# Two blocks on one core: one norm in place of two between the blocks, and other PSUM banks in the mLSTM recurrence

## What is computed

```python
x = x + 0.5 * swiglu_ffn(rmsnorm(x, ffn1_norm), ...)
x = x + hybrid_mixer(rmsnorm(x, mix_norm), ...)
x = x + 0.5 * swiglu_ffn(rmsnorm(x, ffn2_norm), ...)
x = rmsnorm(x, final_norm)                    # end of the first block
h = rms_norm(x, norm_pre_g)                   # start of the second
u_a, z_a, q, k, v, o, z_b, gates, g_a, g_b = split(h @ w_in)
y_a = pooled(u_a) ... * silu(z_a)
h_fwd, h_bwd = mlstm_direction(...), flip(mlstm_direction(flip ...))
y_b = rms(h_fwd + h_bwd) * g * sigmoid(o) * silu(z_b)
merged = sigmoid(g_a + b0) * (y_a @ w_a) + sigmoid(g_b + b1) * (y_b @ w_b)
out = x + rms_norm(merged @ w_out, norm_post_g)
```

## Time and profile before

| | |
|---|---|
| runs, us | 1773.84, 1777.64 (median), 1782.02 |
| profiled execution, us | 1782.81 |
| its span, us | 1780.9 |
| mean granted TensorE clock | 0.969 |
| TensorE matmuls, busy | 1695.4 us, 7980 |
| DVE / ACT / GpSimd busy, us | 691.9 / 628.9 / 655.1 |

### The profile page before, as it was taken

The page is one execution under the profiler, slowest core; times in us unless marked ns, Lnnn a source line. Parts: engine busy times, 40 slices in busy tenths (PEclk is TensorE's granted clock), DMA queues, the critical chain, the costliest instruction groups (busy, mean ns, idle before and its releaser), DMA issues.

```text
span 1780.9 us, 22491 instructions
## 1 busy us (share of the span) xinstructions
PE 1695.4 (95%) x7980; PEld 1386.7 (78%) x7980; DVE 691.9 (39%) x1149; ACT 628.9 (35%) x929; POOL 655.1 (37%) x282
## 2 busy tenths in 40 slices
PE   7999999999999999999999989889888999999997
PEld 6888888888876678888888877667676778887886
DVE  4333330235327644333330127473736332372222
ACT  5322222234136553332222234334343433244432
POOL 3444444443330034444444434222222223444444
PEclk9999999999998899999999989899999999999999
DMA  4322222243220012222222222111111112332222
GB/s 159 105 94 94 96 100 99 95 155 93 71 83 13 1 36 95 95 94 94 94 100 101 95 71 71 61 70 60 59 59 52 66 48 83 118 99 90 95 95 95
DMA packets 41954, 149.25 MB, mean 84 GB/s; under 512 B 4784, under 2 KB 4912, under 8 KB 41648
## 3 DMA queue, kind: packets, MB, share of 16 engines
q1 hardware_dynamic: 40112, 142.36, 23.4%
q10 hardware_dynamic: 1792, 6.19, 1.1%
HBM read 145.39 MB, written 2.10 MB: 83 GB/s over the span
## 4 chain that ended last, share of the span: by engine, by line
PE 69%; issue 22%; POOL 4%; DVE 3%; ACT 1%; DMA 0%; POOLq 0%; DVEq 0%; SPq 0%; ACTq 0%
PE ps L499 15%; PE ps L501 15%; PE ps L500 15%; PE ps L601 4%; PE ps L603 4%; PE ps L602 4%; POOL w_lo L445 4%; PE ps L759 1%; PE ps L771 1%; PE ps L781 1%; PE ps L520 1%; PE ps L1084 1%; PE ps L1083 1%; PE ps L1082 1%; PE ps L527 1%
## 5 line engine op out<-in xcount | busy, mean ns | idle before, releaser
L445 POOL TENSOR_TENSOR w_lo<-w_raw,w_hi 128x1024 fp32r<-128x1024 f32 x262 | 633.9, 2420 | 992.1 <-ACT w_hi L1118 983.9
L1118 ACT ACTIVATE w_hi<-w_raw 128x1024 fp32r<-128x1024 f32 x260 | 275.5, 1060 | 967.5 <-PE ps L501 750.4
L499 PE MATMUL ps<-h_hi,w_hi 128*128 128x512 f32 x1496 | 595.3, 398 | 13.2 <-POOL w_lo L445 8.4
L500 PE MATMUL ps<-h_lo,w_hi 128*128 128x512 f32 x1496 | 586.5, 392 | 0.0
L501 PE MATMUL ps<-h_hi,w_lo 128*128 128x512 f32 x1496 | 586.3, 392 | 0.0
L499 PEld LDWEIGHTS ps<-h_hi,w_hi 128*128 128x128 f32 x1496 | 283.7, 190 | 76.8 <-issue 10.7
L501 PEld LDWEIGHTS ps<-h_hi,w_lo 128*128 128x128 f32 x1496 | 283.4, 189 | 60.2
L500 PEld LDWEIGHTS ps<-h_lo,w_hi 128*128 128x128 f32 x1496 | 283.8, 190 | 58.1
L601 PE MATMUL ps<-hid_hi,w_hi 128*128 (+1 forms) x352 | 137.0, 389 | 0.0
L603 PE MATMUL ps<-hid_hi,w_lo 128*128 (+1 forms) x352 | 136.9, 389 | 0.0
L602 PE MATMUL ps<-hid_lo,w_hi 128*128 (+1 forms) x352 | 136.9, 389 | 0.0
(11 more groups left out here) (303 smaller groups left out, 1679.5 us busy)
## 6 DMA issues: line engine op xcount, KB each, us to landing
w_raw<-in_units SPq DMA_DIRECT2D x262, 512.0 KB, 3.2
x<-in_x SPq DMA_DIRECT2D x4, 512.0 KB, 6.0
w<-in_w ACTq DMA_DIRECT2D x1, 2048.0 KB, 7.7
out<-scr SPq DMA_DIRECT2D x8, 256.0 KB, 2.0
scr<-proj ACTq DMA_DIRECT2D x8, 128.0 KB, 3.0
inv_count<-in_inv_count ACTq DMA_DIRECT2D x1, 1024.0 KB, 4.9
const<-in_const SPq DMA_DIRECT2D x1, 770.0 KB, 9.6
q_sc<-in_row_const ACTq DMA_DIRECT2D x1, 512.0 KB, 3.7
```

Of the source, the lines that this page charges most:

```text
L445: nc.gpsimd.tensor_tensor(w_lo[:, slot, :], w_raw[:, slot, :], w_hi[:, slot, :].bitcast(F32), ALU.subtract).then_inc(w_lo_done, 1)
L499: nc.tensor.matmul(ps[:, bank, :], whi, hi[:, k, :], start=(n == 0), stop=False)
L500: nc.tensor.matmul(ps[:, bank, :], whi, lo[:, k, :], start=False, stop=False)
L1118: nc.scalar.activation(w_hi[:, slot, :], w_raw[:, slot, :], ACT.Copy).then_inc(w_hi_done, 1)
```

## The change

1. **One norm between the blocks.** FFN2 now ends as FFN1 does: its stream is split raw, with the gain `g_both` = final gain times pre gain. The gates unit and four units of head 0 (`NRAW`) run on this raw stream and are multiplied with `r_row` by DVE as they are taken (`raw_take`). Two sums are made at once: of the squares, and of the squares times the final gain squared (in `r_row` as scratch, `add_square`); two column sums in bank 5 follow the first unit of head 0, and `inverse_of_both` makes from them the inverse root of the first norm (`x_col`) and the product of both (`r_col`). The spread of the roots goes into the middle of the next unit (`amid`), into bank 6.
2. **The normalised stream** `n_hi`, `n_lo` is made beside units 2 to 4 through banks 2, 3 and 7: DVE writes the product to PSUM (`stream_part`), ACT casts, DVE subtracts. GpSimd has no part in it. `y_hi`, `y_lo` now share the memory of `h_hi`, `h_lo`.
3. **Head 0** takes its units in the order v, v, o, o, q, q, k, k, z, z (`FIRST_HEAD`), ACT follows `opening_head`, and DVE does all gate rows first, then the four convolutions.
4. **The final gain and `x_col`** are applied to x in `pooled`: ACT scales each chunk before it is turned (`scale_x`) and copies the turned chunk in four quarters, each with its tokens' scale.
5. **Banks of the recurrence.** The state's addition of odd steps goes to banks 2 and 3 (`add_bank`); step n waits for the update of step n-2. The results are turned into banks 6 and 7. The wait for `yb` moves from the turn of keys and values to the scores, which now follow unit 0.

The diff, cut to its core:

```diff
+        def add_bank(n):
+            return 4 if n % 2 == 0 else 2
+        FIRST_HEAD = (4, 5, 6, 7, 0, 1, 2, 3, 8, 9)
+        NRAW = 4
+        STREAM_BANKS = (2, 3, 7)
...
-            tails(U_MIXOUT + 2, U_GATES + 2)
-            pair_sums(4)
-            stream_tails()
-            tails(U_GATES + 2, NUNITS)
+            tails(U_MIXOUT + 2, NUNITS)
...
             def column_sums(n):
                 pe.wait_ge(sqsum_done, n + 1)
...
+                bank = 5 if n == 3 else 0
+                mm = add_squares(bank, 0, scr[:, 0, :], True, True)
+                if n == 3:
+                    mm = add_squares(bank, TT, r_row, False, True)
+                mm.then_inc(ssq_done, 1)
...
-                if sums_inside:
-                    squares_of_half(norm_of + 1, True)
...
             def gates():
-                pe.wait_ge(ssq_done, 5)
-                tile_unit(unit(U_GATES), 4, h_hi, h_lo, stream_tail)
+                pe.wait_ge(x_done, DC * 3 + 5)
+                tile_unit(unit(U_GATES), 4, h_hi, h_lo, raw(3))
+
+            def first_head():
+                for n in range(HEAD_UNITS):
+                    if n == HEAD_UNITS - 1:
+                        turn_rows()
+                    pe.wait_ge(ev_done, n + 1)
+                    un = unit(U_HEADS + n)
+                    if n < NRAW:
+                        tile_unit(un, n % 2, h_hi, h_lo, amid=(lambda: row_of_roots(3)) if n == 1 else None)
+                    else:
+                        tile_unit(un, n % 2, n_hi, n_lo, stream if n == NRAW else None)
+                    if n == 0:
+                        column_sums(3)
...
                 def turn_keys_values():
-                    pe.wait_ge(y_done, Y_FREE + 2 * p)
                     pe.wait_ge(qk_done, 4 * p + 4)
...
+                def head_scores():
+                    pe.wait_ge(y_done, Y_FREE + 2 * p)
                     for c in range(NCH):
...
                         pe.wait_ge(kw_done, 6 * p + n + 1)
-                        if n:
-                            pe.wait_ge(c_done, 6 * p + n)
+                        if n == 1:
+                            pe.wait_ge(qs_done, 2 * p + 2)
+                        elif n:
+                            pe.wait_ge(c_done, 6 * p + n - 1)
                         for e in range(2):
-                            mm = nc.tensor.matmul(ps[:, 4 + e, 0:VW], k_w[:, d, e * P:(e + 1) * P], v_aug[:, c, :],
+                            mm = nc.tensor.matmul(ps[:, add_bank(n) + e, 0:VW], k_w[:, d, e * P:(e + 1) * P], v_aug[:, c, :],
                                                   start=True, stop=True)
...
-                            mm = nc.tensor.transpose(ps[:, 2 + e, c * MC:(c + 1) * MC], h_tok[:, c, e * P:(e + 1) * P], ident)
+                            mm = nc.tensor.transpose(ps[:, 6 + e, c * MC:(c + 1) * MC], h_tok[:, c, e * P:(e + 1) * P], ident)
...
-            ffn(U_FFN2, 1, 2, True)
-            norm(3, "before")
-            norm(4, "last")
+            ffn(U_FFN2, 1, 2)
             gates()
-            mlstm(0, core=False)
+            first_head()
...
             def gates():
+                act.wait_ge(unit_done, U_GATES)
+                act.dma_start(q_sc[:, 1, :, :].rearrange("p a t -> p (a t)"), dram["row_const"]).then_inc(rows_in, 16)
                 head(unit(U_GATES + 2))
...
+                head(unit(U_HEADS + 2))
+                root_of_both()
+                root_row(3)
...
+            def opening_head():
...
+                for n, j in enumerate(FIRST_HEAD):
+                    if n == 1:
+                        for c in range(3):
+                            stream_head(c)
+                    if n == 2:
+                        stream_head(3)
+                        gate_logarithms()
+                    if n:
+                        head(unit(U_HEADS + n + 2))
+                    if n == 2:
+                        for c in range(4, DC):
+                            stream_head(c)
+                    if n == NRAW:
+                        act.wait_ge(ev_done, 2 + NRAW)
+                        for e in range(2):
+                            nc.scalar.activation(merged[:, e, :], merged[:, e, :], ACT.Sigmoid).then_inc(gate_fn_done, 1)
+                    if n >= NRAW:
+                        act.wait_ge(unit_done, U_HEADS + n + 1)
...
+                        nc.scalar.activation(dst, ps[:, n % 2, :], func).then_inc(ev_done, 1)
+                    if n == 5:
+                        row_exponentials()
+                    if n >= 6:
+                        activate(n - 6)
...
+                    scale_x(j + 1)
                     act.wait_ge(xt_ready, j + 1)
-                    nc.scalar.activation(x[:, j, :], ps[:, 4 + j % 4, :], ACT.Copy).then_inc(xt_done, 1)
+                    for tt in range(TT):
+                        at = slice(tt * P, (tt + 1) * P)
+                        ins = nc.scalar.activation(x[:, j, at], ps[:, 4 + j % 4, at], ACT.Copy, scale=x_col[:, tt:tt + 1])
+                    ins.then_inc(xt_done, 1)
...
             def add_square(n, c):
                 dve.wait_ge(sq_done, DC * n + c + 1)
+                if n == 3:
+                    if c == 1:
+                        chain.link(nc.vector.tensor_scalar(r_row[:, :], scr[:, 0, :], g_square[:, 0:1], None, ALU.mult))
+                    chain.link(nc.vector.scalar_tensor_tensor(r_row[:, :], scr[:, c, :], g_square[:, c:c + 1], r_row[:, :],
+                                                              ALU.mult, ALU.add))
                 ins = nc.vector.tensor_tensor(scr[:, 0, :], scr[:, 0, :], scr[:, c, :], ALU.add)
...
+            def stream_part(c):
+                if c >= 3:
+                    dve.wait_ge(hn_lo_done, c - 2)
+                nc.vector.scalar_tensor_tensor(ps[:, STREAM_BANKS[c % 3], :], x[:, c, :], g_both[:, c:c + 1], ps[:, 6, :],
+                                               ALU.mult, ALU.mult).then_inc(hn_done, 1)
...
+            def first_stream():
...
+                inverse_of_both()
+                dve.wait_ge(r_row_done, 4)
+                dve.wait_ge(unit_done, U_GATES + 1)
+                nc.vector.tensor_tensor(rows_of[3], ps[:, 4, :], r_row[:, :], ALU.mult).then_inc(gates_out, 1)
+                raw_take(0)
+                for c in range(DC):
+                    stream_part(c)
+                    if c >= 1:
+                        stream_rest(c - 1)
+                    if c in (3, 6):
+                        raw_take(c // 3)
+                stream_rest(DC - 1)
+                raw_take(3)
...
+                if not core:
+                    gates()
+                    row_ends()
+                    for j in range(4):
+                        convolve(j)
+                    row_columns()
+                    gate_product(0)
+                    gate_product(1)
+                    return
```

More of the change, by code:

```diff
@@ L1009, in mlstm @@
                 for j in range(HEAD_UNITS):
-                    for part in between[j] if core else ():
+                    for part in between[j]:
                         part()
-                    if not core and j == HEAD_UNITS - 1:
-                        turn_rows()
                     project(j)
-                if core and units:
+                if units:
                     turn_outputs()
@@ L1136, in raw_head @@
                     act.wait_ge(x_in[c // 2], 16)
-                nc.scalar.activation(h_hi[:, c, :], x[:, c, :], ACT.Copy, scale=p_(gain, c, c + 1)).then_inc(raw_hi_done, 1)
+                nc.scalar.activation(h_hi[:, c, :], x[:, c, :], ACT.Copy, scale=weight(gain, c)).then_inc(raw_hi_done, 1)
             def root(n):
@@ L1178, in streams @@
                 def streams(lo, hi):
-                    if gain is not None:
-                        for c in range(lo, hi):
-                            raw_head(norm_of + 1, c, gain)
+                    for c in range(lo, hi):
+                        raw_head(norm_of + 1, c, gain)
                 with act.Fori(0, kps // 2) as i:
@@ L1194, in ffn @@
                 load_root()
-                if gain is not None:
-                    streams(4, 8)
-                    head(unit(ud + 2 * kps + 1))
-                    squares(norm_of + 1, 4, 8)
-                else:
-                    squares(norm_of + 1, 4, 8)
-                    head(unit(ud + 2 * kps + 1))
+                streams(4, 8)
+                head(unit(ud + 2 * kps + 1))
+                squares(norm_of + 1, 4, 8)
             def project():
@@ L1443, in mlstm @@
                 for j in range(HEAD_UNITS + 1):
-                    for part in before.get(j, ()) if core else ():
+                    for part in before.get(j, ()):
                         part()
@@ L1546, in _ @@
             to_stream(U_MIXOUT, 2, "g_ffn2")
-            ffn(U_FFN2, 1, 2, None)
-            norm(3, parts=False)
-            squares(4, 0, 8)
-            norm(4)
+            act.wait_ge(both_done, 1)
```

(7 more changed lines are left out.)

204 lines of the change are left out of this document (95 added, 109 removed).

## The result

The changed kernel takes 1734.9 us (median of 4 runs, 1731.77 to 1740.82) against 1777.9 for the kernel before (4 runs, 1773.84 to 1782.02): ratio 0.9762, 95% interval 0.9741 to 0.9784. That is 43.0 us less, where 59.1 had been worked out, and 0.9 us above the upper end of the range. The profiled execution took 1731.77 us, its span is 1730.0; it is the lowest of its four, while the profiled one of the kernel before, 1782.8, stood above all its timed ones. So the spans differ by 50.9 us and the medians by 43.0; a ledger of the two traces has to leave some 8 us to the executions themselves.

The account below looks back on a forecast made before the run. TensorE, busy 95% of the span, was taken as the bound, so only its idle time, lower-clock time and removable work could be won. 17.0 + 27.9 + 14.2 = 59.1 us off gave 1719 us, range 1707 to 1734.

Parts of the forecast that it names:

- The rest, at nothing: Second half of the FFN, `pooled` and GpSimd's work: the added work is covered and costs nothing, else under 1 us each.
- part B: Banks in the recurrence: 27.9 us from removed `c_state` waits and 14.2 from `yb` waits, half clock included.
- part A: Norm and first head: 86.1 us instead of 103.1, a gain of 17.0, from 10 to 23.
- the sum: Norm: TensorE waits 2.0 us for the second sum, or 4.4 if DVE's eighth operation comes behind GpSimd's third tail.
- unit 3: First head: unit 3 waits 1.6 us for GpSimd's `w_lo`, starting at 15.2 instead of 13.6 after the sum.
- unit 4: First head: TensorE waits 2.5 us for DVE's product of unit 2.
- unit 8: First head: TensorE waits 7.5 us for weights behind the row arguments and exponentials, and loses 1.3 more at half clock.
- the turn: First head, before the keys are turned: 2.7 us wait for ACT's last activation, behind unit 9's product.
- the 0.2 at unit 2: First head: unit 2 starts after a wait of 0.2 us, behind the products of the gates and of unit 0.
- DVE takes the wait's place: Rival, chance 0.15: in the recurrence step 2 waits 2 us per head, clock 1.5 more; 14 us less gain, 1733.
- The first head eats part A: Rival, chance 0.12: row arguments later, unit 8 waits 13 us, the sum 4.4; gain 8 us instead of 17, 1728.
- Slower, by the clock: Rival, chance 0.02: in the recurrence, bursts cycling through six banks drop the clock; at 60% half clock, 1808 us.

Follow-up runs that it names:

- a_fill160: The changed kernel plus 160 unused bytes per partition behind `both_col`; ratio 0.9676 to the kernel before, 1720.3 us on its scale.
- b_both: Kernel before with odd state additions in banks 2 and 3, results turned into banks 6 and 7, scores behind unit 0; 1733.4 us, ratio 0.9744.

## Why the prediction was wrong, point by point

**The step that failed is "The rest, at nothing".** It went through the work that the change adds outside the two regions and found cover for all of it. It never asked what the new tensors do to those that stay. They move them against the weights, and 2976 matmuls, on an engine that is busy for 97% of the span and has nothing to hide behind, take 0.0067 us more each: 19.9 us by count, 16.3 recovered in four stretches by one filler, 15.3 in the runs (0.9762 against 0.9676). Without these slow steps the change is at 1720.3 (`a_fill160`), a gain of 57.6 against the 59.1 forecast. That the two are so close is partly luck: part B brought 3.4 us more than its forecast, and part A, on the same reckoning, 4.9 less. The cause is shown in both directions, slower by an unused tensor and faster by another. What the step did go through held: with fast steps the stretch behind the last result is as long as before (297.9 against 297.8 us), scaled `x` and quarter copies included.

**Part A, 17.0 forecast.** From the last down unit to the first turned key the trace has 85.9 us where 86.1 had been summed. Wait by wait: the sum 1.96 (forecast 2.0), unit 3 1.08 (1.6), unit 4 1.43 (2.5), unit 8 6.82 (7.5), the turn 2.30 (2.7); the 0.2 at unit 2 is not there. The waits are 2.9 us under the forecast, and longer stretches at half clock (around the sum, unit 8 and `turn_rows`) and six units with slow steps (144 x 0.0067, up to 1.0) fill that up. In the runs part A is worth less: 57.6 - 45.5 = 12.1 us, where each term is uncertain by 4 to 5, so that 17.0 is not excluded. The 4.8 us by which the profiled `a_fill160` is longer there, and in which DVE meets GpSimd, would be the difference; that is argued, not shown. The prediction had this meeting within 0.2 us and put 4.4 us on the wait (4.17 measured), but "2.4 at most" on the total; with the half clock around it, the stretch was 4.8 longer. The waits seen are 1.9, 2.0 or 4.2 in the five profiles of the changed kernel's family and nothing between. The Trainium skill ("SBUF — State Buffer", "SBUF: two separate sides") has it that whichever of the two engines starts first gets the pair of ports for its whole instruction and blocks the other; the traces agree, with 2.87 us for DVE's addition where it came second and 2.88 for GpSimd's tail where that did. The forecast took the shorter wait, and in the change it came by 0.03 us: luck, too.

**Part B, 42.1 forecast,** came out at 45.5 in the runs and 45.4 in the trace: 16.9 for the results' banks (14.2) and 29.7 for the updates' (27.9), both within their intervals. Heads 2 and 3 of the change are 75.6 and 75.5 us long (75.0 forecast); with fast steps, in `b_both`, 74.3. In the change 39.5 remain; the slow steps on `n` account for 4.3 of the 5.9 lost (291.4 us against 287.1 in `a_fill160`). No wait for `h_sum` came at step 2, and `yb` is waited for in the last head alone.

**The rivals.** Measured at 1734.9, the time lies next to *DVE takes the wait's place* (1733), but nothing of that happened: there is no wait for DVE at step 2. *The first head eats part A* (1728) did not come either in the trace of the change. A case with another mechanism would have been taken for either by its time alone; only the stretches told. *Slower, by the clock* is refuted: with bursts through six banks the granted clock of heads 2 and 3 is 1.00 in both.

```profile
1211.80:1287.40 75.60, 75.50 (x350) 62.29 (x349) 45.52 (x101) 31.57 (x45) 24.02 (x10) 1.00 0.21 70
1287.40:1362.90 75.50, 75.46 (x350) 62.27 (x349) 45.45 (x101) 31.58 (x45) 24.02 (x10) 1.00 0.21 70
```

The Trainium skill ("TensorE: Matmul & The Clock Gate", "A second HAM failure mode: psum-queue depth-cycling") reports an oscillating clock for a kernel that cycles through PSUM banks; this trace does not show it.

**The range** was worked out from the uncertainty of the terms that stood in the sum. The term that was missing lay outside all of them, and it was larger than any of their errors.

## What to carry to other kernels

When a change adds, drops or resizes a tensor, compare the start addresses of all others before and after, and try to keep the distance between the two operands of the hot matmuls at a multiple of 256 bytes, the only distances that were fast here; a filler costs some bytes of memory and no time. (Placing the small tensors behind the large ones should do the same; it was not tried.) When the waits come out as forecast and the time does not, cut both traces at the same places and look first at a stretch that the change does not touch: a difference there at full clock and without waits is in the instructions themselves. A gain is best measured part by part on the kernel before, since two parts of one change can cancel without a trace in the list of waits.

## What the runs showed of the hardware

- A 128x128 by 128x512 matmul of this kernel steps at 0.2267 us at full clock (0.2275 on `n` in `a_fill160`) when its two operands start at a distance that is a multiple of 256 bytes, and at up to 0.2343 when they don't (table above). Even and odd multiples of 256 were both fast. For the operands that are streamed past the weights a distance of 64 cost least (0.2291). Only the distances in the table were tried, and why the distance counts stays open (the trace has weight loads and matmuls on the same memory at the same time).
- Addresses alone did nothing: every tensor 32 bytes higher gives a ratio of 0.9996 (0.9977 to 1.0015).
- A DVE addition of 0.69 us took 2.87 when it began 0.02 us after a GpSimd operation of 2.34 us; where it began 0.03 us ahead it took 0.69 and GpSimd's operation 2.88.
- At the wait of 2.0 us for the sum the granted clock fell to half some 2 us after the wait had ended and stayed there for between 3 and 4 us; at the wait of 4.2 it fell some 1.5 us before the end and stayed for some 10.
